# Gate rows and the mLSTM heads' row of gate sums made by DMA through device memory in place of products with the identity and with ones

## The chip, the core and the metric

The kernel runs on one core of one Trainium2 chip, in float32 throughout. Its engines work side by side, each through its own queue in program order: TensorE (PE, with its weight load PEld), VectorE (DVE), ScalarE (ACT), GpSimd (POOL) and SyncE (SP). They wait for each other by semaphores. The metric is the device time of one execution in microseconds (us). The kernel before takes 2371.95 us, the median of 3 runs (2371.75 to 2374.5).

## What is computed

Two transformer blocks in a row, each with two layers, on 256 tokens of width 1024. Cut to what the change touches:

```python
# first block, layers 0 and 1
ada = silu(c) @ w_ada[l] + b_ada[l]              # one row of 6 x 1024 values
sh1, sc1, g1, sh2, sc2, g2 = split(ada, 6)
h = layer_norm(ALPHA * h + g1 * mixer(u))        # g1 is one row, the same for all tokens
h = layer_norm(ALPHA * h + g2 * swiglu(u))
# in the mixer's mLSTM, per head, per direction
b = cumsum(log_sigmoid(f_pre))                   # over the tokens
log_d = where(tri, b[:, None] - b[None, :] + i_pre[None, :], NEG)
m_t = max(log_d.max(-1), b + m);  s = q @ k.T * exp(log_d - m_t)
# second block: an attention layer ("attn") and a GLA layer ("gla")
x = x + g1 * rms_norm(y);  x = x + g2 * rms_norm(mlp(x))    # attn also with g1x, g2x for the context's 256 tokens
```

Two things are needed in a layout in which they are not made. The gates `g1`, `g2` (`g1x`, `g2x`) are made as columns, 128 partitions by 8 values, and are needed as one row of 1024 values that is the same on all 128 partitions. For the mLSTM, `i - b` (4 heads, 2 directions, 256 tokens) is made with the tokens on the partitions and is needed as a row over the tokens, the same on all partitions.

## The kernel before

All work of the program stands in one SBUF area, `arena`, and eight PSUM banks. It goes through four stages: `layer 0`, `layer 1`, `attn`, `gla`. In each, TensorE runs the projections one panel of weights after the other. SyncE loads the panels (1 MB halves) into a ring of seven, each as soon as TensorE has freed a slot; GpSimd loads the pieces of `w_ada` (1 MB) into two slots, as VectorE uses them up. VectorE makes the gates by products with these pieces (`ada_turn`) between its other work. The order on every engine is written out by hand, and all waits are on counts.

- **Gate rows.** `gate_row` on TensorE (L631 to L639) makes one row: for each half, four 128x128 products of a column, repeated over 128 columns, with the identity `ident`, into one bank. On ScalarE `gate_row` (L1455 to L1460) copies each half from its bank into `grow`. There are ten rows: `g1` and `g2` in each of the two layers, `g1`, `g1x`, `g2`, `g2x` in `attn`, `g1` and `g2` in `gla`.
- **Where they stand on TensorE.** In a layer `g1` comes after the eight QK tiles and ahead of the twelve AQK tiles, `g2` after the tile `W3 10` and ahead of the first `W2` product. In `attn` `g1` and `g1x` come after `VL` and ahead of `RK` (the rotation of the keys), `g2` and `g2x` after panel 6 of the MLP's first half. In `gla` `g1` comes after the transposes `GH 3` and ahead of the wait for their drain by VectorE, `g2` after panel 6 of the MLP.
- **mLSTM heads.** VectorE makes `i - b` and `b` in `aB` (after the tile `CS`, inside its loop over the eight convolutions) and, per head, `make_diag`: four products of the identity with a column of `aB`, 128x128 each. `pe_mini(h, 0)` (L643) multiplies `ones` with the 512 columns of `diag` into the bank `A h`, which is the row on all partitions; the products `S h` follow. `dve_mini(h, 0)` adds the masks to `A h` (128x1024) into `Am`, takes the maximum, and goes on to the probabilities `P h`, which TensorE transposes two AQK tiles later (`PTT h`). Step `s` of head `h` comes after AQK tile `2 h + 1, 3, 4, 5` for `s` = 0, 1, 2, 3.
- **ScalarE in a layer.** It runs one SiLU per convolution (`silu 0` to `silu 7`, L1567 to L1571). VectorE's convolution `n` waits for `silu n-2`, because `cbuf` has two places; `S 0` on TensorE waits for `silu 7`.

## Time and profile before

| | |
|---|---|
| median of 3 runs | 2371.95 us |
| span of the profiled execution, the whole of it that the profile shows | 2375.7 us |
| lowest and highest run | 2371.75, 2374.5 us |
| TensorE busy | 2290.8 us, 96% |
| VectorE busy | 1383.0 us, 58% |
| ScalarE busy | 503.5 us, 21% |
| GpSimd busy | 243.8 us, 10% |
| mean granted TensorE clock | 0.992 of full speed |
| bytes moved by DMA | 391 MB, 165 GB/s |

The profiled execution is one of its own; what lies around the span (start and end of the program) is not in it, and its time as a run is not given apart. A float32 product is two matmul records in the trace, a float32 transpose one, so the number of records of a group is twice the number of its products. The busy time of TensorE is modelled; the distance from the start of one group to the start of the next is the firmer measure of what a group costs.

### The profile page before, as it was taken

How to read it: one execution, taken by the hardware profiler on the slowest of the kernel's cores; microseconds unless marked ns; L12 is line 12 of the kernel's file. 1: busy time of each engine (PE TensorE's matmuls, PEld its weight loads, DVE VectorE, ACT ScalarE, POOL GpSimd, SP SyncE). 2: the span in 40 equal slices, each digit the busy share in tenths (PEclk: the TensorE clock that was granted, in tenths of full speed). 3: DMA queues.
4: the chain of work that ended last, by engine and by line, in shares of the span. 5: the costliest groups of instructions: out<-in, count | busy, mean ns of one | idle time of the engine just before them, and what ended most of it. 6: DMA issues, size and time to landing. Idle time of an engine off the chain costs nothing.

```text
span 2375.7 us, 29622 instructions
## 1 busy us (share of the span) xinstructions
PE 2290.8 (96%) x11910; PEld 1858.6 (78%) x11910; DVE 1383.0 (58%) x2532; ACT 503.5 (21%) x1083; POOL 243.8 (10%) x165
## 2 busy tenths in 40 slices
PE   7999999999999999999999998999999999989998
PEld 5888587799768886868987655588888887767987
DVE  5764334654746433377877666766566457765456
ACT  1222220110011223201011355322200023342200
POOL 0000001321000000013410000000000002001332
PEclk9999999999999999999999999999999999999999
DMA  9853438544475333575564301433333324344442
GB/s 393 329 216 107 159 122 308 193 166 165 179 289 196 107 142 124 193 267 194 195 222 169 109 36 36 138 120 123 133 118 124 115 86 163 124 151 169 157 172 80
DMA packets 163511, 391.34 MB, mean 165 GB/s; under 512 B 6448, under 2 KB 10928, under 8 KB 160560
## 3 DMA queue, kind: packets, MB, share of 16 engines
q1 hardware_dynamic: 136736, 285.03, 33.8%
q0 software_dynamic: 24080, 93.69, 11.0%
q10 hardware_dynamic: 2560, 10.72, 1.3%
q8 instruction: 96, 1.57, 0.3%
q14 instruction: 39, 0.32, 0.0%
HBM read 388.37 MB, written 1.05 MB: 164 GB/s over the span
## 4 chain that ended last, share of the span: by engine, by line
PE 87%; DVE 7%; ACT 2%; DMA 2%; issue 1%; SPq 0%; DVEq 0%; ACTq 0%
PE bank L548 86%; DVE arena L2088 3%; DVE arena L2094 2%; DMA arena<-in_w_ada 2%; PE bank L546 1%; ACT arena L1440 1%; ACT arena L1443 1%; DVE arena L2091 1%; DVE junk L2094 1%; DVE arena L2226 0%; DVE arena L3040 0%; SPq L3202 0%; SPq L3205 0%; ACT L1440 0%; DVE arena L2157 0%
## 5 line engine op out<-in xcount | busy, mean ns | idle before, releaser
L548 PE MATMUL bank<-arena 128*128 128x256 f32 (+5 forms) x11422 | 2235.4, 364 | 46.8 <-DVE arena L2088 17.8
L548 PEld LDWEIGHTS bank<-arena 128*128 128x128 f32 (+2 forms) x11422 | 1801.8, 190 | 467.5 <-issue 250.5
L2088 DVE TENSOR_TENSOR arena<-arena 128x1024 f32<-128x1024 f32 (+8 forms) x535 | 446.6, 849 | 237.2 <-PE bank L548 195.8
L1440 ACT ACTIVATE arena<-arena 128x512 f32<-128x512 f32 (+5 forms) x427 | 213.9, 522 | 811.5 <-DVE arena L2088 458.1
L2094 DVE SCALAR_TENSOR_TENSOR arena<-arena 128x1028 f32<-128x1028 f32 (+6 forms) x367 | 309.2, 859 | 97.0 <-DMA arena<-in_w_ada 76.7
L3280 POOL DMA_DIRECT2D arena<-in_w_ada x88 | 62.9, 715 | 1749.2 <-DVEq L2103 1728.5
L2088 DVE TENSOR_TENSOR arena<-arena,bank 128x256 f32<-128x256 f32 (+2 forms) x326 | 150.1, 485 | 157.4 <-PE bank L548 147.7
L1443 ACT ACTIVATE arena<-bank 128x512 f32<-128x512 f32 (+1 forms) x199 | 110.5, 596 | 462.9 <-PE bank L548 402.3
L2088 DVE TENSOR_TENSOR arena<-bank,arena 128x512 f32<-128x512 f32 (+3 forms) x103 | 69.7, 690 | 215.3 <-PE bank L548 193.3
L1440 ACT ACTIVATE arena<-bank 128x256 f32<-128x256 f32 (+1 forms) x121 | 50.2, 432 | 507.8 <-PE bank L548 507.1
L2094 DVE SCALAR_TENSOR_TENSOR arena<-bank,arena 128x254 f32<-128x254 f32 (+2 forms) x184 | 78.2, 469 | 51.1 <-PE bank L546 34.1
L2091 DVE TENSOR_SCALAR arena<-arena 128x512 f32<-128x512 f32 (+8 forms) x278 | 80.4, 322 | 20.7 <-ACT arena L1440 12.7
L546 PE MATMUL bank<-arena 128*128 128x128 f32 x488 | 64.1, 281 | 28.2 <-DVE arena L2091 16.9
L546 PEld LDWEIGHTS bank<-arena 128*128 128x128 f32 x488 | 57.4, 145 | 39.2 <-issue 22.9
L2094 DVE SCALAR_TENSOR_TENSOR junk<-arena 128x1028 bf16<-128x1028 f32 x64 | 78.7, 1229 | 14.5 <-DMA arena<-in_w_ada 10.1
L2094 DVE SCALAR_TENSOR_TENSOR arena<-arena,bank 128x512 f32<-128x512 f32 (+1 forms) x40 | 24.8, 645 | 99.1 <-PE bank L548 97.3
L1440 ACT ACTIVATE arena<-bank,arena 128x128 f32<-128x128 f32 (+2 forms) x138 | 57.5, 488 | 79.2 <-DVE arena L2088 24.4
L2091 DVE TENSOR_SCALAR arena<-bank,arena 128x256 f32<-128x256 f32 (+1 forms) x112 | 46.5, 468 | 47.2 <-PE bank L548 35.7
L3235 POOL TENSOR_TENSOR arena<-arena 128x1024 f32<-128x1024 f32 x20 | 50.7, 2535 | 116.7 <-PE bank L548 93.8
L1440 ACT ACT_TABLE_LOAD x48 | 61.6, 1283 | 4.2 <-PE bank L548 2.2
L3237 POOL TENSOR_TENSOR arena<-arena 128x1024 f32<-128x1024 f32 x20 | 53.0, 2649 | 1.6
L3250 POOL TENSOR_TENSOR arena<-arena 128x1024 f32<-128x1024 f32 x14 | 33.0, 2355 | 97.6 <-PE bank L548 82.3
(37 smaller groups left out, 222.2 us busy)
## 6 DMA issues: line engine op xcount, KB each, us to landing
arena<-in_w_ada POOLq DMA_DIRECT2D x88, 1028.0 KB, 5.6
arena<-in_w_in SPq DMA_DIRECT2D x84, 1024.0 KB, 7.3
arena<-in_w SPq DMA_DIRECT2D x56, 1024.0 KB, 6.4
arena<-in_w_mlp_in SPq DMA_DIRECT2D x32, 1024.0 KB, 6.5
arena<-in_w_mlp_out SPq DMA_DIRECT2D x32, 1024.0 KB, 6.4
arena<-in_w_gla SPq DMA_DIRECT2D x12, 1024.0 KB, 7.0
arena<-in_w_ada SPq DMA_DIRECT2D x16, 514.0 KB, 19.5
arena<-in_w_a SPq DMA_DIRECT2D x8, 1024.0 KB, 7.0
```

What stands on the lines that cost most here:

```text
L546: ins = nc.tensor.transpose(out, lhsT, rhs)
L548: ins = nc.tensor.matmul(out, lhsT, rhs, start=start, stop=stop)
L1440: return nc.scalar.activation(out, x, f, **kw)
L1443: return nc.scalar.activation(out, tile(key)[:, :out.free_size()], f)
L2088: return V.tensor_tensor(out, x, y, op)
L2091: return V.tensor_scalar(out, x, s1, s2, op0, op1) if op1 is not None else V.tensor_scalar(out, x, s1, None, op0)
L2094: return V.scalar_tensor_tensor(out=out, in0=x, scalar=s, in1=y, op0=op0, op1=op1, **kw)
L3235: nc.gpsimd.tensor_tensor(up_sum(at), a21, a22, ALU.add).then_inc(up_sums_made, 1)
L3237: nc.gpsimd.tensor_tensor(a21, a11, a21, ALU.subtract).then_inc(up_sums_made, 1)
L3250: nc.gpsimd.tensor_tensor(wsum, a21, a22, ALU.add).then_inc(mlp_sums_made, 1)
L3280: pool.dma_start(adaw[:, n % ADA_SLOTS], half_source(job, q)).then_inc(ada_in[n % ADA_SLOTS], 16)
```

## The change

The ten `gate_row`s are gone from TensorE and ScalarE, and so are `make_diag`, `diag` and the eight products with `ones`. In their place ScalarE's queue issues DMAs:

- `row_to_dram` stores the columns of a gate, 128 partitions by 8 values, into a row of `gate_rows` in device memory, as 1024 pieces of 4 bytes.
- `row_to_all`, later on the same queue, waits until that has landed and loads the row of 4 KB into all 128 partitions of `grow` (512 KB).
- For the mLSTM one DMA stores 16 columns of `aB` (2048 pieces of 4 bytes) into `decay_rows` after `silu 2`. After `silu 4` ScalarE waits for its landing and loads the 8 KB into all partitions of `DR` (1 MB), which lies in the area of `VA`. `aB` is laid out so that its first half is those 16 columns.

VectorE waits for `decay_in` ahead of the first head, adds the masks to `DR` in place of the bank, and waits for `row_in` where it waited for ScalarE's drains.

```diff
@@ -333,7 +346,8 @@
 
         gz = area(M["GATE"], NT, 16)
         gw = area(M["GATE"] + 32, 4, 32)
-        aB = area(M["GATE"] + 160, 2, 2, NT, 4)
+        aB = area(M["GATE"] + 160, 2, M_HEADS, 2 * NT).rearrange("p a h (d t) -> p a d t h", d=2)
+        decay_cols = area(M["GATE"] + 160, 4 * M_HEADS)
         small = area(M["GATE"] + 192, 16, 4)
         var, newton = area(M["GATE"] + 240, NT), area(M["GATE"] + 242, NT)
         W = M["WORK"]
...
-            def gate_row(key, cols, stage=None):
-
-                for half in range(2):
-                    ps = open_tile(f"{key} {half}")
-                    pe.wait_ge(dve_of[stage or Progress.phase], DV.of(stage or Progress.phase, "next " + key if stage else key))
-                    for j in range(4):
-                        col = cols[:, 4 * half + j:4 * half + j + 1]
-                        mm(ps[:, j * P:j * P + P], col.to_broadcast([P, P]), ident, done=f"{key} {half}" if j == 3 else None)
-
             def pe_mini(h, s):
 
                 if s == 0:
-                    pe.wait_ge(dve_done, DV.at(f"diag {h}"))
-                    ps = open_tile(f"A {h}")
-                    mm(ps[:, :], ones, diag[:, :, :].rearrange("p a b -> p (a b)"), done=f"A {h}")
                     pe.wait_ge(act_done, AC.at("silu 7"))
                     ps = open_tile(f"S {h}")
...
 
-            def gate_row(key, x):
-
-                for half in range(2):
-                    act.wait_ge(pe_done, PE.at(f"{key} {half} full"))
-                    drain(f"{key} {half}", grow[:, x, PW * half:PW * half + PW]).then_inc(
-                        act_done, AC.drained(f"{key} {half}"))
+            def row_to_dram(stage, key, cols, made_in=None):
+
+                act.wait_ge(dve_of[made_in or stage], DV.of(made_in or stage, "next " + key if made_in else key))
+                act.dma_start(gate_rows[GATE_ROWS.index((stage, key))].rearrange("(k p) -> p k", p=P), cols,
+                              allow_slow_non_contiguous=True).then_inc(row_out, 16)
+
+            def row_to_all(stage, key, x, last=None):
+
+                act.wait_ge(row_out, rows_by(stage, last or key))
+                act.dma_start(grow[:, x, :], gate_rows[GATE_ROWS.index((stage, key))].partition_broadcast(P)).then_inc(row_in, 16)
 
             def context_root(tt):
@@ -1564,12 +1555,20 @@
                 func(gw[:, 1, :], gw[:, 0, :], ACT.Exp, scale=-1.0).then_inc(act_done, AC.step())
                 act.wait_ge(act_done, AC.count)
                 func(gw[:, 2, :], gw[:, 1, :], ACT.Ln, bias=1.0).then_inc(act_done, AC.step("softplus"))
+                row_to_dram(stage, "g1", adac[:, 2, :])
                 for n in range(8):
                     act.wait_ge(dve_done, DV.at(f"conv {n}"))
                     func(QK[:, 2 * n:2 * n + 2, :].rearrange("p a b -> p (a b)"),
                         cbuf[:, 2 * (n % 2):2 * (n % 2) + 2, :].rearrange("p a b -> p (a b)"), ACT.Silu).then_inc(
                         act_done, AC.step(f"silu {n}"))
-                gate_row("g1", 0)
+                    if n == 2:
+                        act.wait_ge(dve_done, DV.at("decays"))
+                        act.dma_start(decay_rows[l].rearrange("(c p) -> p c", p=P), decay_cols,
+                                      allow_slow_non_contiguous=True).then_inc(decay_out, 16)
+                    if n == 4:
+                        row_to_all(stage, "g1", 0)
+                        act.wait_ge(decay_out, 16 * (l + 1))
+                        act.dma_start(DR.rearrange("p h s -> p (h s)"), decay_rows[l].partition_broadcast(P)).then_inc(decay_in, 16)
                 for n in range(12):
                     x, m = (AQ, n) if n < 6 else (AK, n - 6)
...
+                    if p == 1:
+                        row_to_dram(stage, "g2", adac[:, 5, :])
+                    if p == 3:
+                        row_to_all(stage, "g2", 1)
                 act.wait_ge(dve_done, DV.at("up 3"))
                 act.wait_ge(pe_done, PE.at("W1 10 full"))
                 drain("W1 10", sg[:, 2, :], ACT.Silu).then_inc(act_done, AC.drained("W1 10"))
-                gate_row("g2", 1)
 
...
                         context_root(tt)
+                    row_to_dram("attn", "g1", adac[:, 2, :], stage)
+                    row_to_dram("attn", "g1x", adacx[:, 2, :], stage)
                 first_product(0)
                 if l == DEPTH - 1:
...
-            gate_row("g1", 0)
-            gate_row("g1x", 1)
+            row_to_all("attn", "g1", 0, "g1x")
+            row_to_all("attn", "g1x", 1)
 
...
             def attn_extra(p):
+                if p == 4:
+                    row_to_dram("attn", "g2", adac[:, 5, :])
+                    row_to_dram("attn", "g2x", adacx[:, 5, :])
                 if p == 6:
-                    gate_row("g2", 0)
-                    gate_row("g2x", 1)
+                    row_to_all("attn", "g2", 0, "g2x")
+                    row_to_all("attn", "g2x", 1)
 
...
+            row_to_dram("gla", "g1", adac[:, 2, :])
             gk(0)
             gq(0)
             for h in range(G_HEADS):
+                if h == 1:
+                    row_to_all("gla", "g1", 0)
                 if h + 1 < G_HEADS:
                     gk(h + 1)
...
             gg(3)
-            gate_row("g1", 0)
...
+                if p == 4:
+                    row_to_dram("gla", "g2", adac[:, 5, :])
                 if p == 6:
-                    gate_row("g2", 1)
+                    row_to_all("gla", "g2", 1)
 
...
-            def make_diag(h):
-
-                if h:
-                    dve.wait_ge(pe_done, PE.at(f"A {h - 1} full"))
-                for j in range(4):
-                    ts(diag[:, j, :], ident, aB[:, 0, j // 2, j % 2, h:h + 1], None, ALU.mult).then_inc(
-                        dve_done, DV.step(f"diag {h}" if j == 3 else None))
-
             def dve_mini(h, s):
 
                 if s == 0:
-                    dve.wait_ge(pe_done, PE.at(f"A {h} full"))
-                    ps = tile(f"A {h}")
-                    row = ps[:, :].rearrange("p (d s) -> p d s", d=2).unsqueeze(2).to_broadcast([P, 2, NT, T])
-                    tt_(Am[:, :, :, :], row, masks[:, :, :, :], ALU.add).then_inc(dve_done, DV.drained(f"A {h}"))
+                    dve.wait_ge(dve_done, DV.count)
+                    row = DR[:, h, :].rearrange("p (d s) -> p d s", d=2).unsqueeze(2).to_broadcast([P, 2, NT, T])
+                    tt_(Am[:, :, :, :], row, masks[:, :, :, :], ALU.add).then_inc(dve_done, DV.step())
                     dve.wait_ge(dve_done, DV.count)
                     V.reduce_max(small[:, 0, :].rearrange("p (d t) -> p d t", d=2), Am[:, :, :, :], AX.X).then_inc(
                         dve_done, DV.step())
...
-                    if h + 1 < M_HEADS:
-                        make_diag(h + 1)
                     dve.wait_ge(pe_done, PE.at(f"S {h} full"))
                     ps = tile(f"S {h}")
                     dve.wait_ge(act_done, AC.at(f"exp {h}"))
...
+                        marks[Progress.phase, "dve", "decays"] = DV.count
                     if turns[0] < 20:
                         ada_turn(turns.pop(0), [("ada", 0)])
                 if l == 0:
@@ -2631,9 +2632,8 @@
                         tt_(crow[:, i, :D], crow[:, i, :D], csig[i], ALU.mult).then_inc(
                             dve_done, DV.step("conds" if i == 2 else None))
                     dve.wait_ge(masks_in, 16)
-                dve.wait_ge(dve_done, DV.count)
-                make_diag(0)
                 dve.wait_ge(act_done, AC.at("silu 7"))
+                dve.wait_ge(decay_in, 16 * (l + 1))
                 for n in range(12):
...
+                dve.wait_ge(row_in, rows_by(stage, "g1"))
                 for half in range(2):
...
-                dve.wait_ge(act_done, AC.at("g2 1 drained"))
+                dve.wait_ge(row_in, rows_by(stage, "g2"))
```

## Rows read from the trace of the kernel before

**Rows 1.** The page: busy time of each engine; the chain that ended last, by engine.
```profile
PE 2290.8 (96%) x11910; PEld 1858.6 (78%) x11910; DVE 1383.0 (58%) x2532; ACT 503.5 (21%) x1083; POOL 243.8 (10%) x165
PE 87%; DVE 7%; ACT 2%; DMA 2%; issue 1%; SPq 0%; DVEq 0%; ACTq 0%
```
**Rows 2.** The chain, in order of time: start us, us, what, number of records.
```profile
185.85 18.19 PE bank L548 x82
204.04 0.87 PE bank L546 x8
...
223.97 15.59 PE bank L548 x72
...
1195.99 93.00 PE bank L548 x522
...
1308.39 35.88 PE bank L548 x178
...
1552.37 192.25 PE bank L548 x896
...
2184.20 82.47 PE bank L548 x736
```
**Rows 3.** Timeline of ScalarE, attn: first and last of four half rows; idle, releaser last.
```profile
1333.88 0.60 ACT L1443 ACTIVATE arena<-bank 128x512 f32<-128x512 f32 x1 [0.29 <-PE bank L548]
...
1336.56 0.60 ACT L1443 ACTIVATE arena<-bank 128x512 f32<-128x512 f32 x1 [0.29 <-PE bank L548]
```
**Rows 4.** Timeline of VectorE, attn: its last gate product, the rotated keys.
```profile
1334.93 0.08 DVE L2094 DVE_READ_ACCUMULATOR arena<-arena 128x1 f32 x1
1337.48 0.69 DVE L2088 TENSOR_TENSOR arena<-bank,arena 128x512 f32<-128x512 f32 x1 [2.47 <-PE bank L548]
```
**Rows 5.** Timelines of ScalarE and VectorE, gla: g1's last half, post row, GH 3's drain.
```profile
2128.97 0.60 ACT L1443 ACTIVATE arena<-bank 128x512 f32<-128x512 f32 x1 [0.29 <-PE bank L548]
2128.98 0.34 ACTq L2065 DMA_DIRECT2D arena<-in_post  x1
...
2127.38 0.88 DVE L2094 SCALAR_TENSOR_TENSOR arena<-bank,arena 128x256 f32<-128x256 f32 x2 [3.07 <-ACT arena L1443]
```
**Rows 6.** Timeline of ScalarE, layer 0: silu 2, 4, 5, 7; drain of AQK 1.
```profile
104.29 0.63 ACT L1440 ACTIVATE arena<-arena 128x512 f32<-128x512 f32 x1 [7.50 <-DVE arena L2094]
...
118.58 0.63 ACT L1440 ACTIVATE arena<-arena 128x512 f32<-128x512 f32 x1 [6.52 <-DVE arena L2094]
125.73 0.63 ACT L1440 ACTIVATE arena<-arena 128x512 f32<-128x512 f32 x1 [6.52 <-DVE arena L2094]
...
140.04 0.63 ACT L1440 ACTIVATE arena<-arena 128x512 f32<-128x512 f32 x1 [6.52 <-DVE arena L2094]
...
149.94 0.66 ACT L1440 ACTIVATE arena<-bank 128x256 f32<-128x256 f32 x2 [6.27 <-PE bank L548]
```
**Rows 7.** Timelines of VectorE and PE, layer 0: convolution 7, Am, P 0, PTT 0.
```profile
135.38 1.00 DVE L2091 TENSOR_SCALAR arena<-bank,arena 128x256 f32<-128x256 f32 x2 [0.23 <-DVE arena L2094]
...
150.87 1.23 DVE L2088 TENSOR_TENSOR arena<-bank,arena 128x1024 f32<-128x1024 f32 x1 [5.07 <-PE bank L548]
...
158.34 0.88 DVE L2094 SCALAR_TENSOR_TENSOR arena<-arena 128x256 f32<-128x256 f32 x2
...
166.19 0.60 PE L546 MATMUL bank<-arena 128*128 128x128 f32 x4
```
**Rows 8.** The page: DMA queues (packets, MB, share of 16 engines); issues, us to landing.
```profile
q1 hardware_dynamic: 136736, 285.03, 33.8%
q0 software_dynamic: 24080, 93.69, 11.0%
...
arena<-in_w_in SPq DMA_DIRECT2D x84, 1024.0 KB, 7.3
...
arena<-in_small SPq DMA_DIRECT2D x1, 29.0 KB, 20.0
```
**Rows 9.** Windows, layer 0: busy PE, PEld, DVE, ACT, POOL; clock, DMA share, GB/s.
```profile
110.00:120.00 10.00, 10.00 (x47) 8.71 (x47) 9.60 (x21) 1.26 (x2) 0.71 (x1) 1.00 0.95 370
```

More of the change, by code:

```diff
@@ L212, in minis, with rows_by @@
     return [(h, s) for h in range(M_HEADS) for s, lag in ((3, 5), (2, 4), (1, 3), (0, 1)) if n == 2 * h + lag]
+GATE_ROWS = [("layer 0", "g1"), ("layer 0", "g2"), ("layer 1", "g1"), ("layer 1", "g2"), ("attn", "g1"), ("attn", "g1x"),
+             ("attn", "g2"), ("attn", "g2x"), ("gla", "g1"), ("gla", "g2")]
+def rows_by(stage, key):
+    return 16 * (GATE_ROWS.index((stage, key)) + 1)
 class Progress:
@@ L276, in program @@
         small_in, par2_in = sem("small_in"), sem("par2_in")
+        row_out, row_in = sem("row_out"), sem("row_in")
+        decay_out, decay_in = sem("decay_out"), sem("decay_in")
+        gate_rows = nc.dram_tensor("gate_rows", (len(GATE_ROWS), D), F32).ap()
+        decay_rows = nc.dram_tensor("decay_rows", (DEPTH, 4 * PW), F32).ap()
         PE, AC, DV = (Progress(n, marks) for n in ("pe", "act", "dve"))
@@ L343, in program @@
         hn = area(W + 2048, NT, T)
-        diag = area(W + 2560, 4, P)
+        DR = area(M["VA"], M_HEADS, PW)
         cbuf = area(W, 4, T)
@@ L1120, in _ @@
             release(w_kv)
-            gate_row("g1", adac[:, 2, :], last)
-            gate_row("g1x", adacx[:, 2, :], last)
             pe.wait_ge(par2_in, 16)
@@ L1255, in attn_seam @@
                 evicted("Y", range(2, 4))
[L1257 to L1262 removed]
+            fast_mlp("mlp", 0, T, attn_seam)
             normed_transposes("next", dg_next, range(2), None)
@@ L2863, in fast_mlp @@
                         tiles_, rows_used, sem_, count, _, _ = post
-                        dve.wait_ge(act_done, AC.at("g2x 1 drained" if tiles_ == 4 else "g2 1 drained"))
+                        dve.wait_ge(row_in, rows_by(Progress.phase, "g2x" if tiles_ == 4 else "g2"))
                         dve.wait_ge(sem_, count)
@@ L2992, in _ @@
                 ada_turn(q, [("ada", 1), ("adax", 2)])
-            dve.wait_ge(act_done, AC.at("g1x 1 drained"))
+            dve.wait_ge(row_in, rows_by("attn", "g1x"))
             dve.wait_ge(dve_done, DV.count)
@@ L3174, in _ @@
                         dve_done, DV.drained(f"GH {h}" if ft else None))
-            dve.wait_ge(act_done, AC.at("g1 1 drained"))
+            dve.wait_ge(row_in, rows_by("gla", "g1"))
             dve.wait_ge(dve_done, DV.count)
```

16 lines of the change are left out of this document (2 added, 14 removed).

## Prediction

> **What bounds the kernel now.** I read the busy times first: TensorE is busy 96% of the span, VectorE 58%, ScalarE 21%, and the chain that ended last lies on TensorE for 87% of its length and on DMA for 2% [rows 1]. Then the chain in order of time, to see whether TensorE leads at the places that the change touches [rows 2]. It does in long unbroken pieces. The pairs 18.19 + 0.87 are the mLSTM heads, the 93.00 us from 1195.99 hold layer 1's `g2`, the 35.88 us from 1308.39 hold `g1` and `g1x` of attn, the 192.25 us from 1552.37 `g2` and `g2x`, and the 82.47 us from 2184.20 gla's `g2`. A product taken out of such a piece shortens the run by its whole time, unless whoever is waited for next was just on time. That is what the timelines are read for.
>
> **What the change removes.** *Price of a gate row.* A half row is four products of 128x128. In attn four halves run one behind the other; ScalarE drains them as they come, at 1333.88 and so on to 1336.56 [rows 3], so a half takes (1336.56 - 1333.88) / 3 = 0.893 us and a row 1.79 us. *Price of a product with `ones`.* A piece of the heads with no such product has 72 records in 15.59 us, 0.2165 us each; the piece with one has 82 records in 18.19 us, of which 80 are of the same kind [rows 2]. 18.19 - 80 x 0.2165 = 0.87 us. There are eight, four heads in two layers: 6.96 us.
>
> *Which rows come back whole.* In the layers four rows, 7.15 us. Layer 0's `g1` stands between QK and AQK: `silu 7` is over at 140.67 and `S 0`, the first to need it, follows AQK 1, drained at 149.94 [rows 6], so TensorE can come 1.79 us earlier and meets nobody. `g2` of layer 1 stands in 93.00 us of TensorE alone, which run on over the first half of the down products [rows 2]; layer 0 runs the same code with less on VectorE. In attn four rows, 7.15 us. `g1`, `g1x` are followed by `RK`; VectorE ends its gate products at 1334.93 + 0.08 and then waits 2.47 us, until 1337.48, for `RK` [rows 4]. Without the rows `RK` is there at some 1333.9, VectorE starts on it at 1335.0, and TensorE goes on with query 0, which needs neither; the 3.57 us come back whole. `g2`, `g2x` lie inside 192.25 us of TensorE alone [rows 2]. gla's `g2`, 1.79 us, likewise.
>
> *Which does not.* gla's `g1` hides a wait. VectorE drains `GH 3` from 2127.38 to 2128.26, and the last half of `g1` is full at 2128.97 [rows 5]. TensorE then needs `GH 3`. With the row gone it waits until 2128.3 in place of 2128.95: 0.65 us of the 1.79 come back. The load of the post row, issued at 2128.98, moves ahead of the two drains, and nothing else follows.
>
> Sum: nine rows at 1.79 (16.1), one at 0.65, eight products at 0.87 (6.96): **23.7 us**. ScalarE also loses twenty drains of 0.60 us, beside TensorE, so nothing. VectorE loses 32 products for `diag`, beside TensorE as well. Its addition of the masks, 1.23 us [rows 7], reads SBUF in place of a bank; I take it unchanged. It may start before `S h`, which only adds slack.
>
> **What the change adds.** *Loads to all partitions.* Twelve, ten of 0.5 MB and two of 1 MB, 7 MB against 391 MB. On ScalarE a load of this kind costs 0.34 us of issue [rows 5], and it lands like a panel, in 7.3 us [rows 8]. Every user comes tens of us later (`row_in` is waited for at the first residual or late in the MLP). Nothing. They share the DMA engines with the weights at shares up to 0.95 [rows 9], but the panel ring is seven deep and TensorE shows no wait for it. The chain has 2% on DMA [rows 1], the pieces of `w_ada`; 7 MB more is 1.8% more bytes, so 0 to 1 us. I take 0.
>
> *Stores in pieces of 4 bytes.* No row shows such a store. Its issue on ScalarE costs 0.34 us [rows 5] at least, and at most as long as the store takes. Its landing I bound from packets. The queue of the panels had 136736 packets in 33.8% of 16 engines' 2375.7 us, 0.094 us each; the software queue 24080 in 11.0%, 0.174 us each [rows 8]. The gate sums are 2048 pieces, 128 an engine. Low end: a panel of 1 MB, 7.3 us. At 0.094 us a piece: 12 us. High end, where each piece waits for one packet of either other queue: 128 x 0.36 = 46 us. I take 12 us, since the share of the engines at the time leaves gaps, and keep 46. Below nothing it can't be: it replaces no transfer.
>
> *The new wait.* Behind it on ScalarE stand `silu 5` to `silu 7`, and behind these VectorE's convolutions and `S 0`. The store is issued at the end of `silu 2`, 104.9; ScalarE gets to the wait at 119.2, after `silu 4`; `silu 5` comes at 125.73 [rows 6]. A landing within 14 us costs nothing at all. Convolution 7 starts at 135.38 [rows 7] and needs `silu 5`; with 0.63 us for it and two issues, ScalarE may wait until some 134, 29 us after the store. After that convolution 7 and `silu 7` slip, and `silu 7` has from 140.67 to about 148.1 (149.94 less 1.8), 7.5 us more. So TensorE loses only what the landing takes **beyond 36.7 us**. The load into `DR` then lands at about 149, and `P 0` takes from 150.87 to 159.22 and is wanted at 166.19 [rows 7], 2.7 us earlier in the changed kernel: later than this, so it does not bind first. Layer 1 has the same loop; I take the same slack. At 12 us the cost is 0, at 46 us 2 x 9.3 = 18.6 us.
>
> The gate rows' stores are half as many pieces and are waited for two silus or two MLP panels later or more: never late where the other is not. Issued on ScalarE, they stand ahead of work with several us of idle time before it, as the 6.52 us before each SiLU [rows 6].
>
> The Trainium skill, page "Perfetto Trace Analysis", section "DMA Optimizations", speaks against the stores: DMAs under 2 KB have a significant overhead each. No row here shows one; with the high end of 46 us the time would be 2366.9 us. The page "DMA: Bandwidth & Descriptors", section "Measured (HBM→SBUF, 128 partitions, SWDGE, issued from GpSimd)", has about 10.5 ns for a small packet; an estimate by it is 1.3 us over a fixed part for 128, which leaves the sum at 23.7.
>
> Profiled execution: 2375.7 - 23.7 = 2352.0. It lies 3.7 us above the median of the runs, and I take that offset as unchanged: 2371.95 - 23.7 = **2348.3 us**.
>
> **The rivals.** *A, the gain is partly swallowed at seams.* Where attn and gla hand over between the halves of an MLP, the chain passes through VectorE, and if VectorE leads there, the four rows of attn and gla's `g2` come back as waits: 5 x 1.79 = 8.9 us less, 2357.2. For it: 7% of the chain is VectorE's [rows 1]. Against it: it waits 2.47 us right behind `g1x` [rows 4], and `g2` lies in unbroken TensorE time.
>
> *B, the stores are slow, but bearable.* Landing between 36.7 and 48 us, or an issue that holds ScalarE as long in gla's heads, where it is in the chain: up to all of the gain, in the middle about 2360. For it: a load of only 29 KB took 20.0 us to land behind others [rows 8], and the engines are 95% busy just then [rows 9]. Against it: that load stood behind a start-up queue on its own ring.
>
> *C, slower than before: the wait for `decay_out` stops ScalarE, and TensorE waits at `S 0` for `silu 7`, in both layers.* Price 2 x (landing - 36.7). It eats the 23.7 us at a landing of 48.5 us, 0.38 us a piece, and decides for slower from there; at 0.47 us a piece (60 us) the time is 2371.95 - 23.7 + 46.6 = 2394.9. For it: the engines' share of 0.95 at the wait [rows 9]; against it: it needs more than one packet of each other queue between any two pieces.
> By the Trainium skill, "DMA: Bandwidth & Descriptors", section "Queues, rings and completion order", an engine goes round the queues and takes a whole packet from each; were every piece a packet of its own among full queues, that is the high end of 46 us, short of C.
>
> **How the numbers follow.** Forecast 0.75 (2344 to 2352 by itself, for the rounding of the prices and 0 to 1 us of DMA), A 0.10, B 0.10, C 0.05. The range from 2344 to 2358 holds the forecast, A and about a third of B, with the rest of B and C left out. A measurement of this kernel can tell some 0.2% from no change, 4.7 us. Faster by more: forecast, A and most of B, 0.92. Within: 0.03, the end of B. Slower: C and nothing else, 0.05.
>
> **What would show it.** Right: TensorE has 176 fewer records (160 of the rows, 16 with 512 columns), its busy time is down by some 23 us and its idle time up by 1 us at most; the head period falls from 19.06 to 18.2 us; ScalarE reaches `silu 5` within a few us of `silu 4`; VectorE's first addition of masks in a layer no longer waits for a bank; in gla TensorE idles 1.1 us before the first mix tile. Wrong: a gap of ScalarE between `silu 4` and `silu 5` of over 15 us, TensorE idle before `S 0` (B, C); TensorE idle growing at the seams of attn or before `scores 0` (A); long DMA issues on ScalarE's queue.

## The result, and the profile after

The changed kernel takes **2359.11 us** (median of 5 executions, 2356.3 to 2364.93) against 2373.25 us before (5 executions): a ratio of 0.9945, 95% interval 0.9934 to 0.9956. By the ratio it is faster by 13.1 us (10.4 to 15.7), by the two medians by 14.1, and not by the 23.7 of the forecast; 2359.11 lies 1.1 us above the range.

The page after, busy times and waits of TensorE (us in total, how many, the longest). (Lines have moved: L562, L560 are the products of L548, L546; VectorE's L2099, L2102, L2105 are L2088, L2091, L2094; ScalarE's L1427, L1430 are L1440, L1443.)

```profile
span 2357.3 us, 29223 instructions
PE 2267.6 (96%) x11734; PEld 1838.6 (78%) x11734; DVE 1375.0 (58%) x2500; ACT 492.3 (21%) x1063; POOL 243.4 (10%) x165
...
PE bank L562 <- DVE arena L2099: 17.4, 11, 3.0
...
PE bank L560 <- DVE arena L2099: 3.9, 1, 3.9
```

TensorE has 176 records fewer and is busy 23.2 us less than in [rows 1]. Its idle time, span less busy, went from 84.9 to 89.7 us. The wait of 3.9 us is new. It is in gla's first head; the chain of the kernel before runs there on TensorE for 92.92 us on end, and the chain after goes another way. Start, us and what, first before, then after:

```profile
1950.25 92.92 PE bank L548 x392
```
```profile
2000.70 2.40 DVE arena L2105 x4
...
2003.44 13.13 DMA arena<-in_w_ada
...
2016.60 2.40 DVE arena L2105 x4
...
2025.74 1.09 PE bank L560 x4
```

The timelines of ScalarE's queue, GpSimd, VectorE and TensorE at this place (start, us, and in brackets the idle time before), after and then, of GpSimd and VectorE, before:

```profile
1998.47 0.38 ACTq L1445 DMA_DIRECT2D gate_rows<-arena  x1
...
2000.91 0.72 POOL L3281 DMA_DIRECT2D arena<-in_w_ada  x1 [11.23 <-DVEq L2114]
...
2012.95 1.23 DVE L2105 SCALAR_TENSOR_TENSOR arena<-arena 128x1028 f32<-128x1028 f32 x1 [9.87 <-DMA arena<-in_w_ada]
...
2016.60 1.23 DVE L2105 SCALAR_TENSOR_TENSOR arena<-arena 128x1028 f32<-128x1028 f32 x1 [1.26 <-DMA arena<-in_w_ada]
...
2025.74 1.79 PE L560 MATMUL bank<-arena 128*128 128x128 f32 x6 [3.93 <-DVE arena L2099]
```
```profile
2022.27 0.72 POOL L3280 DMA_DIRECT2D arena<-in_w_ada  x1 [11.23 <-DVEq L2103]
...
2027.50 1.23 DVE L2094 SCALAR_TENSOR_TENSOR arena<-arena 128x1028 f32<-128x1028 f32 x1 [3.06 <-DMA arena<-in_w_ada]
...
2030.35 1.23 DVE L2094 SCALAR_TENSOR_TENSOR arena<-arena 128x1028 f32<-128x1028 f32 x1 [0.46 <-DMA arena<-in_w_ada]
```

ScalarE stores gla's `g1` at 1998.47. The piece of `w_ada` that GpSimd asks for 2.4 us later is there only at 2012.93, 12.0 us after its issue; in the kernel before the same piece took 5.2 us (issued 2022.27, there at 2027.48). VectorE stands still for 9.87 us instead of 3.06, and for the next piece 1.26 instead of 0.46, so its part of head 0 is late, and TensorE waits.

What the DMA engines did meanwhile, by windows (us, busy PE, PEld, DVE, ACT, POOL; clock, DMA share, GB/s). First the kernel after: the store, the time behind it, and the recovery; then the kernel before with its piece:

```profile
1999.00:2001.00 2.00, 2.00 (x6) 0.81 (x5) 1.85 (x5) 0.00 (x0) 0.09 (x1) 1.00 0.24 2
...
2004.00:2010.00 6.00, 6.00 (x29) 5.28 (x28) 0.00 (x0) 0.38 (x1) 0.16 (x1) 1.00 0.73 38
2010.00:2014.00 4.00, 4.00 (x20) 3.52 (x19) 1.05 (x1) 0.00 (x0) 0.00 (x0) 1.00 0.95 381
```
```profile
2025.00:2029.00 4.00, 4.00 (x20) 3.51 (x19) 1.50 (x3) 0.39 (x1) 0.52 (x1) 1.00 1.02 407
```

The packets of the store itself are over by 2001: the queue view from 1998 to 2004 has 1040 of them (1024 pieces and 16 more of 4 bytes) in 8.0% of 16 engines' 6 us, 0.007 us each. Yet from 2004 to 2010 the engines are "busy" for 0.73 of the time and move 38 GB/s, a tenth of the 407 that they move in the kernel before at full share. A high share does not say that bytes flow: from 2004 to 2010 there are 56 read packets in 73.1% of 16 engines' 6 us, 1.25 us each, where one of the kernel before takes 0.16 from 2025 to 2029. The same stands behind the larger store of the gate sums in layer 0, which lands at 116.25, after and then before:

```profile
110.00:116.00 6.00, 6.00 (x29) 5.23 (x29) 5.13 (x11) 0.63 (x1) 0.71 (x1) 1.00 0.78 34
116.00:120.00 4.00, 4.00 (x21) 3.48 (x20) 3.50 (x8) 0.36 (x1) 0.00 (x0) 1.00 0.93 306
```
```profile
110.00:116.00 6.00, 6.00 (x29) 5.23 (x29) 5.67 (x13) 0.63 (x1) 0.71 (x1) 1.00 1.03 405
```

So here the reads are slow until the store has landed, and fast again right behind it. For gla's store the trace of the changed kernel has no landing; that of `gates_only`, the kernel below with the ten rows' DMAs alone, has one. The store is issued at 2007.54, its packets are over by 2010, and it lands at 2017.63, 10.1 us after its issue. The windows before and behind that:

```profile
2014.00:2017.60 3.60, 3.60 (x19) 3.16 (x18) 0.00 (x0) 0.06 (x1) 0.00 (x0) 1.00 0.90 35
...
2020.00:2022.00 2.00, 2.00 (x11) 1.77 (x10) 0.00 (x0) 0.00 (x0) 0.00 (x0) 1.00 0.97 380
```

In layer 0 the slow reads cost TensorE nothing. ScalarE's timeline, layer 0, answers [rows 6]:

```profile
119.64 0.63 ACT L1427 ACTIVATE arena<-arena 128x512 f32<-128x512 f32 x1 [7.16 <-DVE arena L2105]
119.65 0.34 ACTq L1451 DMA_DIRECT2D arena<-gate_rows  x1
120.03 0.46 ACTq L1571 DMA_DIRECT2D arena<-decay_rows  x1
130.42 0.63 ACT L1427 ACTIVATE arena<-arena 128x512 f32<-128x512 f32 x1 [10.14 <-DVE arena L2105]
```

The load into `DR` is issued right behind `silu 4`: the new wait for `decay_out` cost nothing, the store had landed 11.5 us after its issue. The load itself takes 13.6 us, not the 7.3 of the forecast, and still lands long before it is needed. `silu 5` is 3.6 us further from `silu 4` than before, because VectorE waited 3.52 us for a piece of `w_ada`. `silu 7`, at 145.2, is still ahead of `S 0`.

**A figure used below.** Executions differ in mean granted clock, and the time follows it: over 44 executions of the kernel before, beside all the runs below, the time rises by 2.4 us for each 0.001 that the mean clock is lower. So beside the median the table gives the *time at full clock*, time less (1 - mean clock) x span, median over the executions. The clock of an execution is given to 0.001, 2.4 us, so this figure scatters by 1 to 2 us from one execution to the next.

| kernel | executions | median us | ratio to before (95%) | mean clock | at full clock | TensorE's gap in gla's head 0 |
|---|---|---|---|---|---|---|
| before | 44 | 2372.2 | 1 | 0.9934 | 2357.3 | none |
| changed, both series | 11 | 2361.8 | 0.9945, 0.9949 | 0.9907 | 2339.9 | 3.9; 5.5 |
| `gates_only` | 5 | 2362.9 | 0.9966 (0.9954 to 0.9978) | 0.9910 | 2342.8 | 4.0 |
| `row_only` | 12 | 2368.3 | 0.9983 (0.9975 to 0.9992) | 0.9930 | 2351.1 | none |
| `no_stores` | 4 | 2350.4 | 0.9912 (0.9899 to 0.9925) | 0.9928 | 2334.1 | none |
| `gla_g1_no_store` | 6 | 2352.4 | 0.9910 (0.9893 to 0.9927) | 0.9920 | 2334.0 | none |
| `gla_g1_late` | 4 | 2351.3 | 0.9910 (0.9893 to 0.9926) | 0.9922 | 2333.7 | none |
| `packed`, `packed_again` | 9 | 2352.9 | 0.9917, 0.9922 | 0.9914 | 2332.0 | none |
| `packed_gates` | 4 | 2353.9 | 0.9921 (0.9906 to 0.9936) | 0.9912 | 2332.7 | none |
| pieces 8, 16, 32, 64 bytes apart | 18 | 2351.6 | 0.9909, 0.9908, 0.9913, 0.9903 | 0.9925 | 2333.9 | none |
| `one_partition` | 5 | 2361.0 | 0.9948 (0.9932 to 0.9964) | 0.9916 | 2340.7 | 1.0 |
| `double` | 6 | 2406.5 | 1.0124 (1.0096 to 1.0153) | 0.9830 | 2363.5 | 17.0 |

### The profile page after: what moved, and what is told of

Same layout as the page of the kernel before. It is cut to its first block, busy times and chain, and to the rows that moved or that the text cites. A ratio compares the mean times of both kernels' runs of the same rounds, so it can differ in the third digit from the quotient of the medians.

```text
span 2357.3 us, 29223 instructions
## 1 busy us (share of the span) xinstructions
PE 2267.6 (96%) x11734; PEld 1838.6 (78%) x11734; DVE 1375.0 (58%) x2500; ACT 492.3 (21%) x1063; POOL 243.4 (10%) x165
## 4 chain that ended last, share of the span: by engine, by line
PE 87%; DVE 8%; ACT 2%; DMA 1%; issue 1%; SPq 0%; DVEq 0%; ACTq 0%
PE bank L562 85%; DVE arena L2099 4%; DVE arena L2105 3%; PE bank L560 1%; DMA arena<-in_w_ada 1%; ACT arena L1427 1%; ACT arena L1430 1%; DVE junk L2105 1%; DVE arena L2102 1%; DVE arena L3041 1%; DVE arena L2237 0%; ACT L1427 0%; SPq L3203 0%; DVE arena L2168 0%; SPq L3195 0%
## 5 line engine op out<-in xcount | busy, mean ns | idle before, releaser
L562 PE MATMUL bank<-arena 128*128 128x256 f32 (+5 forms) x11246 | 2211.2, 365 | 49.1 <-DVE arena L2099 17.4
L562 PEld LDWEIGHTS bank<-arena 128*128 128x128 f32 (+2 forms) x11246 | 1781.4, 190 | 466.2 <-issue 248.0
L2099 DVE TENSOR_TENSOR arena<-arena 128x1024 f32<-128x1024 f32 (+7 forms) x543 | 455.0, 853 | 231.5 <-PE bank L562 186.1
L1427 ACT ACTIVATE arena<-arena 128x512 f32<-128x512 f32 (+5 forms) x427 | 213.7, 522 | 811.1 <-DVE arena L2099 464.0
L2105 DVE SCALAR_TENSOR_TENSOR arena<-arena 128x1028 f32<-128x1028 f32 (+6 forms) x367 | 309.0, 859 | 105.2 <-DMA arena<-in_w_ada 85.8
L2099 DVE TENSOR_TENSOR arena<-arena,bank 128x256 f32<-128x256 f32 (+2 forms) x326 | 150.1, 485 | 157.9 <-PE bank L562 148.5
L1430 ACT ACTIVATE arena<-bank 128x512 f32<-128x512 f32 (+1 forms) x179 | 99.4, 596 | 451.1 <-PE bank L562 407.3
L2099 DVE TENSOR_TENSOR arena<-bank,arena 128x512 f32<-128x512 f32 (+2 forms) x95 | 59.9, 645 | 173.7 <-PE bank L562 154.9
L1427 ACT ACTIVATE arena<-bank 128x256 f32<-128x256 f32 (+1 forms) x121 | 50.2, 432 | 508.2 <-PE bank L562 507.5
L2105 DVE SCALAR_TENSOR_TENSOR arena<-bank,arena 128x254 f32<-128x254 f32 (+2 forms) x184 | 78.1, 469 | 73.4 <-PE bank L560 34.1
L560 PE MATMUL bank<-arena 128*128 128x128 f32 x488 | 65.0, 283 | 31.0 <-DVE arena L2102 16.6
L560 PEld LDWEIGHTS bank<-arena 128*128 128x128 f32 x488 | 57.8, 146 | 42.5 <-issue 21.4
L2105 DVE SCALAR_TENSOR_TENSOR junk<-arena 128x1028 bf16<-128x1028 f32 x64 | 78.7, 1229 | 13.9 <-DMA arena<-in_w_ada 9.6
L2102 DVE TENSOR_SCALAR arena<-arena 128x256 f32<-128x256 f32 (+8 forms) x246 | 74.0, 327 | 19.3 <-ACT arena L1427 12.7
L2105 DVE SCALAR_TENSOR_TENSOR arena<-arena,bank 128x512 f32<-128x512 f32 (+1 forms) x40 | 24.8, 645 | 99.7 <-PE bank L562 97.9
L2102 DVE TENSOR_SCALAR arena<-bank,arena 128x256 f32<-128x256 f32 (+1 forms) x112 | 46.5, 468 | 51.3 <-PE bank L562 38.1
L1427 ACT ACTIVATE arena<-bank,arena 128x128 f32<-128x128 f32 (+2 forms) x138 | 57.5, 486 | 83.8 <-PE bank L560 23.7
```

The lines of the kernel that those rows point to most:

```text
L560: ins = nc.tensor.transpose(out, lhsT, rhs)
L562: ins = nc.tensor.matmul(out, lhsT, rhs, start=start, stop=stop)
L1427: return nc.scalar.activation(out, x, f, **kw)
L1430: return nc.scalar.activation(out, tile(key)[:, :out.free_size()], f)
L2099: return V.tensor_tensor(out, x, y, op)
L2102: return V.tensor_scalar(out, x, s1, s2, op0, op1) if op1 is not None else V.tensor_scalar(out, x, s1, None, op0)
```

## The experiments

Theory S: a store in pieces of 4 bytes slows the reads from device memory behind it, and who waits for those is late. Its rivals are the loads to all partitions, the layers, and a long profiled execution of before.

**One part alone.** `gates_only` keeps the diagonals and the products with `ones` and has no DMA of the gate sums; `row_only` is the kernel before with those products in DMAs, and the ten rows on TensorE. Of `gates_only`:

```diff
+                    mm(ps[:, :], ones, diag[:, :, :].rearrange("p a b -> p (a b)"), done=f"A {h}")
...
-                        act.dma_start(decay_rows[l].rearrange("(c p) -> p c", p=P), decay_cols,
```

> The ten gate rows by DMA, the mLSTM row left on TensorE with its diagonals. Theory S (the stores in pieces of 4 bytes slow the DMA reads that follow them for some 10 us, and what waits for those reads is late): the ten rows take 17.8 us of TensorE away, and the gap of 3.9 us in gla's first head with what follows it gives 4 to 6.5 us back, so 2373.3 - 17.8 + 5 = about 2360 to 2362, and VectorE still waits about 10 us for a piece of w_ada in gla. Theory R (the missing gain is spent in the layers, at the mLSTM row's load and the later SiLUs): about 2355.5, with all the gain of the ten rows.

> Only the mLSTM row by DMA, the ten gate rows left on TensorE and ScalarE. Theory S: the eight products come back whole, 6.9 us, since nothing on TensorE waits for the slowed reads in the layers: about 2366.4. Theory R: 2370 or more, with TensorE idle in the layers.

Measured: `gates_only` 2362.9, with VectorE's wait at 10.7 us and the gap at 4.0. (The 17.8 us of the expectation are ten rows at 1.78; the prediction gave the ten 16.7, as gla's `g1` comes back by 0.65 alone.) `row_only` 2368.3, 3.6 us under before by the medians and 6.2 at full clock, for 6.9 forecast. So the layers do not eat the gain, and the shortfall comes with the gate rows. The two do not add up exactly: at full clock `gates_only` gains 14.5 us and `row_only` 6.2, 20.7 together, where the changed kernel has 17.4; what makes the 3.3 us is open.

**Without stores, and with one store left out.** `no_stores` has no store at all; `gla_g1_no_store` lacks the line `row_to_dram("gla", "g1", ...)` alone, and its load reads attn's row. Of `no_stores`:

```diff
-                act.dma_start(gate_rows[...].rearrange("(k p) -> p k", p=P), cols, ...)
-                act.wait_ge(row_out, ...)
+                act.dma_start(grow[:, x, :], a["post"][x].partition_broadcast(P)).then_inc(row_in, 16)
```

> The changed kernel without any store of gates or of gate sums; its loads to all partitions stay, at the same places, and read inputs of the same size, so the values are not the reference's. Theory S: the pieces of w_ada in gla land in 5.4 us again instead of 12, TensorE's gap in gla's first head is gone, and the time is 2352.5 to 2355. Theory L (the loads to all partitions, 7 MB, are what costs): no change, 2359. Theory O (the gain is smaller only because the profiled execution of before was a long one): no change, 2359.

> The changed kernel without one store, that of gla's g1; the load takes attn's g1 row, so the values are not the reference's. If this store alone costs (theory S with its place: two pieces of w_ada land in 12 to 13 us instead of 5.4, VectorE is 9.9 us late, TensorE idles 3.9 us in gla's first head and the clock falls there): 4 to 7 us less than the changed kernel, 2352 to 2355. If the other nine stores and the two of the gate sums take as much: 2 us less or none, 2357 to 2359.

> The changed kernel once more, beside the next three, for the spread of its executions and their mean granted clock. If the clock is lower in it than in the kernel before by more than chance, it is near 0.991 again (0.9935 is the mean of 17 executions of before) and the time near 2359; if the first five executions fell low by chance, the mean clock comes to 0.993 and the time to about 2355.

Measured: without any store 2350.4, 8.7 us under the changed kernel and a little under the expected 2352.5 to 2355, with all twelve loads in place; so the loads cost nothing that shows (23.2 us gained at full clock, 23.7 forecast). With the one store of gla's `g1` left out and the other eleven there, 2352.4, beside 2363.2 of the changed kernel in the same series: 10.8 us hang on this store. The changed kernel's second series had the clock of the first (0.9907 and 0.9908), and its gap was 5.5 us behind a wait of VectorE of

```profile
2019.73 1.23 DVE L2105 SCALAR_TENSOR_TENSOR arena<-arena 128x1028 f32<-128x1028 f32 x1 [11.86 <-DMA arena<-in_w_ada]
```

**The same store at another time.**

```diff
-            row_to_dram("gla", "g1", adac[:, 2, :])
             gk(0)
...
                 if h == 1:
-                    row_to_all("gla", "g1", 0)
+                    row_to_dram("gla", "g1", adac[:, 2, :])
+                if h == 3:
+                    row_to_all("gla", "g1", 0)
```

> The changed kernel with one store moved: gla's g1 is stored at head 1 (some 33 us later) and loaded at head 3. Nothing else differs and the values are the reference's. Theory S with its place: the reads are slowed for 10 us at a time in which VectorE waits for no piece of w_ada, so the 3.9 to 5.5 us of TensorE's gap and the lower clock around it are gone: 2352 to 2355, as without that store. If the store costs wherever it stands: 2359 to 2363.

Measured: 2351.3, slightly under the expected range. The store comes 36 us later and costs nothing there, as GpSimd loads the next piece only 8.7 us later (in 5.9 us) and VectorE is not waiting for it. VectorE's wait at the old place:

```profile
2009.10 1.23 DVE L2106 SCALAR_TENSOR_TENSOR arena<-arena 128x1028 f32<-128x1028 f32 x1 [3.18 <-DMA arena<-in_w_ada]
```

**Twice as many pieces.** Each store once more, into rows of its own.

> Every store in pieces of 4 bytes twice, the second into rows of its own. Theory S with a price for each piece (about 6.6 us of delay for 1024 pieces): the pieces of w_ada in gla land in 18 to 22 us, TensorE idles 10 to 14 us in gla's first head, the gate sums land in 20 to 24 us and the layers lose 0 to 5 us each: 2368 to 2380. If a store costs a fixed time whatever its pieces or overlaps itself: 2359 to 2362.

Measured: 2406.5, far above the expected 2368 to 2380. In gla the step is as expected: a first piece of `w_ada` in 23.9 us, VectorE's wait, TensorE's gap, and the window behind the stores with 29 GB/s:

```profile
2045.48 1.23 DVE L2109 SCALAR_TENSOR_TENSOR arena<-arena 128x1028 f32<-128x1028 f32 x1 [21.72 <-DMA arena<-in_w_ada]
...
2059.46 1.79 PE L560 MATMUL bank<-arena 128*128 128x128 f32 x6 [16.97 <-DVE arena L2103]
...
2025.00:2042.00 17.00, 17.00 (x66) 12.02 (x64) 0.00 (x0) 0.38 (x1) 0.00 (x0) 1.00 0.86 29
```

What was not expected is ScalarE's queue in layer 0, and TensorE's wait for it:

```profile
108.71 0.37 ACTq L1568 DMA_DIRECT2D decay_rows<-arena  x1
109.11 11.94 ACTq L1570 DMA_DIRECT2D decay_rows<-arena  x1
...
123.43 21.12 ACTq L1453 DMA_DIRECT2D arena<-gate_rows  x1
...
154.84 1.15 ACT L1427 ACTIVATE arena<-arena 128x512 f32<-128x512 f32 x2 [30.79 <-DMA decay_rows<-arena]
...
160.93 14.45 PE L562 MATMUL bank<-arena 128*128 128x256 f32 x59 [10.79 <-ACT arena L1427]
```

The second store's issue holds ScalarE for 11.94 us and the next DMA's for 21.12, the second store lands after 45.3 us, and this is the forecast's rival C at work. The reads do not slow down there: the 4096 pieces go out between the packets of the others, from 112 to 156, and the engines move 320 GB/s and more from 120 to 150; the pieces of `w_ada` land in 10.4 to 11.2 us.

```profile
130.00:140.00 10.00, 10.00 (x47) 8.72 (x47) 9.61 (x20) 0.00 (x0) 0.71 (x1) 1.00 1.02 325
```

So the number of pieces alone does not slow the reads. In gla the 2048 are out within 2.5 us of their issue, in layer 0 of the changed kernel within 8; whether it is this burst that makes the difference, no run varied alone. The clock falls with the pauses, to 0.983 in the mean, and that alone makes 25 us against before: (0.9934 - 0.9830) x 2390.

**As many pieces, further apart.** The columns of the target are spread: its last dimension is 16 for pieces 64 bytes apart, and 8, 4 and 2 for 32, 16 and 8 bytes. The loads read inputs, as in `no_stores`; in gla the load comes over 40 us after the store, so this does not touch the piece behind it.

```diff
-        gate_rows = nc.dram_tensor("gate_rows", (len(GATE_ROWS), D), F32).ap()
+        gate_rows = nc.dram_tensor("gate_rows", (len(GATE_ROWS), D, 16), F32).ap()
```

> As many pieces of 4 bytes, issued at the same places, but each 64 bytes from the next in device memory; the loads read inputs of the same size, so the values are not the reference's. If the slowing comes with the number of pieces: 2357 to 2360, pieces of w_ada in 12 us in gla as in the changed kernel. If it comes from neighbouring pieces that are written into the same stretch of device memory by different engines: like the kernel without stores, 2350 to 2353, and w_ada in 5.4 us.

> As the run with pieces 64 bytes apart, but 32 bytes apart: two pieces of 4 bytes in each 64 bytes. The loads read inputs, so the values are not the reference's. If what costs is that several pieces fall into one stretch of 64 bytes, already two of them: pieces of w_ada in gla over 8 us, time 2354 to 2360. If it grows with the number of pieces in a stretch (16 in the changed kernel, 2 here), or the stretch is of 32 bytes or less: pieces of w_ada within 6.5 us and 2350 to 2354.

> Pieces of 4 bytes 16 bytes apart, four in each 64 bytes; the loads read inputs, so the values are not the reference's. If the slowing grows with the number of pieces in a stretch (16 in the changed kernel gave 6.6 to 8.6 us more on a w_ada piece, 2 gave none): between 0 and 3 us more, time 2350 to 2354. If there is a threshold between 16 and 32 bytes: as the changed kernel, pieces of w_ada in 12 us, 2359.

> Pieces of 4 bytes 8 bytes apart, eight in each 64 bytes; the loads read inputs, so the values are not the reference's. If the slowing grows with the number of pieces in a stretch: a piece of w_ada in gla in 7 to 10 us, VectorE's wait for it 5 to 7 us, time 2352 to 2358. If only pieces that touch each other are slow: 5.4 us and 2350 to 2354.

Measured: 2352.2, 2351.2, 2350.9, 2350.5. Still 1024 pieces of 4 bytes each, and in gla no slow reads down to 16 bytes (5.3 to 5.5 us for the piece of `w_ada`; in layer 0, behind 2048 pieces, 9.2 to 9.7, for 8.2 in `packed` and before). VectorE's wait in gla for pieces 64, 32, 16 and 8 bytes apart:

```profile
2005.69 1.23 DVE L2105 SCALAR_TENSOR_TENSOR arena<-arena 128x1028 f32<-128x1028 f32 x1 [3.31 <-DMA arena<-in_w_ada]
...
2002.49 1.23 DVE L2105 SCALAR_TENSOR_TENSOR arena<-arena 128x1028 f32<-128x1028 f32 x1 [3.18 <-DMA arena<-in_w_ada]
...
2004.80 1.23 DVE L2105 SCALAR_TENSOR_TENSOR arena<-arena 128x1028 f32<-128x1028 f32 x1 [3.11 <-DMA arena<-in_w_ada]
...
2008.01 1.23 DVE L2105 SCALAR_TENSOR_TENSOR arena<-arena 128x1028 f32<-128x1028 f32 x1 [4.32 <-DMA arena<-in_w_ada]
```

At 8 bytes it begins (the piece of `w_ada` in 6.5 us in gla and 12.4 in layer 0; 6.5 in gla for itself says little, `row_only` has it there with no store), at 4 bytes, side by side, it is 12.0 and 14.0 us. The stores themselves land sooner too: 2048 gate sums 16 bytes apart in 5.7 and 6.0 us, 8 bytes apart in 7.9 and 9.2, side by side in 11.5 and 12.5 (13.4 twice in the second series).

**Who writes the neighbours.** The pieces stay 4 bytes and side by side, but the 8 (or 16) neighbours come from one partition:

```diff
-                ...rearrange("(k p) -> p k", p=P), cols, ...
+                ...rearrange("(p k) -> p k", p=P), flat48[:, at:at + 16:2], ...
```

> As many pieces of 4 bytes as in the changed kernel, into as few bytes of device memory, but neighbours come from one partition: each partition writes its 8 (or 16) values side by side, taken from every other column so that each stays a piece of its own; the values are not the reference's. If the slowing comes from different DMA engines writing next to each other at the same time: 2350 to 2354, pieces of w_ada in under 6.5 us in gla. If it comes from many pieces in one stretch of device memory, whoever writes them: 2357 to 2363, 12 us or more.

Measured: 2361.0. In gla the piece takes 9.6 us and the gap is 1.0; in layer 0 the two pieces behind the store take 21.7 and 18.8 (15.8 and 15.6 in the changed kernel, 18.6 and 18.8 in its second series), VectorE waits 7.3 us, and TensorE 2.8 us for ScalarE. So that different partitions write next to each other is not the whole of it; neither expectation is met in full.

The landing of the store orders all of these. In gla, us from the issue to the landing:

| gla's `g1` store | the store | the piece of `w_ada` issued 2.4 us behind it |
|---|---|---|
| `packed`, 128 pieces of 32 bytes | 1.4 | 5.4 |
| 64, 32, 16 bytes apart | 2.7, 2.6, 3.2 | 5.5, 5.3, 5.3 |
| 8 bytes apart | 4.8 | 6.5 |
| `one_partition` | 7.3 | 9.6 |
| `gates_only`, side by side | 10.1 | 12.9 |

Where the store takes longer than 4 us, the piece lands 4.1 to 5.2 us behind it. What keeps a store open for so long after its packets is not shown; and layer 0 of `double`, with fast reads beside a store that is open for 45 us, says that an open store is not enough by itself.

**Fewer, whole pieces.** The rows of `w_ada` that make the gates are laid out so that partition `p` holds the values 8p to 8p + 7; a gate goes out as 128 pieces of 32 bytes, the gate sums as 128 of 64, and VectorE reads `DR` with a stride. `packed_gates` does it for the gates alone.

```diff
-                act.dma_start(gate_rows[...].rearrange("(k p) -> p k", p=P), cols, ...)
+                act.dma_start(gate_rows[...].rearrange("(p k) -> p k", p=P), cols)
-                        act.dma_start(decay_rows[l].rearrange("(c p) -> p c", p=P), decay_cols, ...)
+                        act.dma_start(decay_rows[l].rearrange("(p c) -> p c", p=P), decay_cols)
```

> The same DMAs with whole pieces for each partition: the rows of w_ada that make the gates are laid out so that a partition's eight values are neighbours (128 pieces of 32 bytes), and the gate sums are stored 64 bytes a partition and read by VectorE with a stride, in two additions a head. Theory S, by the number of pieces: like the kernel without stores, 2352.5 to 2355.5, w_ada pieces in 5.4 to 6 us in gla. If the slowing comes with any store to device memory, whatever its pieces: 2359. If the strided addition is dear: VectorE's additions of the masks take over 2 us in place of 1.23, still beside TensorE.

> The gate rows stored as 128 pieces of 32 bytes, the gate sums in pieces of 4 bytes as in the changed kernel. If the stores of the gate sums cost the run nothing (rivals B and C off): as with everything packed, 2352 to 2354, and silu 7 still 4 to 5 us late in both layers. If they cost through the pieces of w_ada and the SiLUs of the layers: 2355 to 2359.

> The kernel with pieces of 32 and 64 bytes once more, for its spread and mean clock. 2351 to 2354; mean clock 0.9915 to 0.9925 if the clock is lower without the gate rows on TensorE for another reason than the slowed reads, 0.993 or more if the first four executions were low by chance (then 2349).

Measured: 2352.6, 2353.9 and 2353.6. `packed` is the better version that the runs point to, with `gla_g1_late` beside it: both beat both kernels, and their difference is within the spread. Gate sums land in 2.1 us (2.5 and 2.7 in `packed_again`), and VectorE's two strided additions take 1.95 us, beside TensorE:

```profile
144.40 1.95 DVE L2097 TENSOR_TENSOR arena<-arena 128x512 f32<-128x512 f32 x2
```

`packed_gates` has `silu 7` at 145.1 as the changed kernel has, and no loss: the slowed reads of the layers cost the run nothing.

## Why the prediction was wrong, and where it was right

**The removal was right.** At full clock the kernels without the slowed reads of gla stand at 2333.7 (45 executions; 2332.0 to 2334.1 by the rows of the table), 23.6 us under before; the forecast was 23.7. The pieces of the chain after show the prices of products with `ones`, against 18.19 in [rows 2]:

```profile
164.57 17.33 PE bank L562 x80
181.90 0.87 PE bank L560 x8
```

18.19 - 17.33 = 0.86 a head, forecast 0.87, and a head period of 18.20. The pieces with gate rows, again against [rows 2]:

```profile
1181.65 92.84 PE bank L562 x506
...
1294.25 33.94 PE bank L562 x146
...
1535.20 187.00 PE bank L562 x864
...
2167.91 80.68 PE bank L562 x720
```

gla's `g2` gives 82.47 - 80.68 = 1.79, as forecast. The others seem to give 0.16, 1.94 and 5.25 for forecasts of 1.79, 3.57 and 3.57. The windows tell why (columns as above), the kernel after and then before, at the starts of these pieces:

```profile
1182.00:1186.00 4.00, 4.00 (x23) 4.00 (x23) 1.99 (x4) 0.42 (x1) 3.92 (x2) 0.58 0.13 51
1294.50:1298.50 4.00, 4.00 (x23) 4.00 (x23) 0.83 (x4) 2.24 (x7) 0.00 (x0) 0.57 0.00 0
```
```profile
1196.00:1200.00 4.00, 4.00 (x36) 4.00 (x37) 3.39 (x7) 0.84 (x2) 3.90 (x2) 1.00 0.23 93
1308.50:1312.50 4.00, 4.00 (x34) 3.96 (x35) 1.16 (x6) 2.91 (x9) 0.00 (x0) 1.00 0.00 0
1553.50:1557.50 4.00, 4.00 (x12) 3.17 (x12) 3.86 (x4) 0.00 (x0) 0.00 (x0) 0.57 0.00 0
```

After a pause of 2.5 us the clock stands at 1.2 GHz for 3.4 us, which costs 1.7: in the first two pieces of after, in the third of before. With 1.7 added or taken off they give 1.9, 3.6 and 3.5. In gla, `g1` hid VectorE's drain as told: TensorE now idles 1.16 us there, forecast 1.1. Rival A is off; the waits at the seams are those of before (17.4 us in 11 waits, 17.8 before).

**The landing came out right by luck.** Taken 12 us, measured 11.5 and 12.5. The sum took 0.094 us for a piece, from a queue of large packets; the store's own packets take 0.015 us each (2064 in 15.4% of 16 engines' 12.5 us, from 104.5 to 117) and in gla 0.007. At that rate the 128 pieces of an engine are 2 us. In layer 0 the last of them is over 8.0 us after the issue, and the landing comes 3.5 us later still. The wait for `decay_out` cost nothing, as forecast. The price of the wait beyond 36.7 us has one test, and not a clean one, as the issues hold ScalarE too, `double`: landings of 45.3 and 39.2 us give 8.6 + 2.5 = 11.1 us by that rule; TensorE's waits for ScalarE's L1427 grew by 20.5 - 7.3 = 13.2.

**The step that failed** is "Stores in pieces of 4 bytes". It priced the store by who waits for *it*, bounded by how long its own packets queue, and said of the gate rows' stores "never late where the other is not". It did not ask what the store does to the others. The notes on the loads had looked for the panel ring and found it seven deep; the pieces of `w_ada` have two slots, and that VectorE waits 3.06 us for such a piece in gla's head 0 already before the change was not looked up. In its place the runs showed 3.9 and 5.5 us of TensorE's time there, and 10.8 us of the whole on this one store. That head had 3.7 us of room: 6.8 and 0.8 us more of VectorE's waits for two pieces became 3.9 us of TensorE's. The sentence on the loads, "The chain has 2% on DMA", had the same blind spot: it priced bytes. The store's own place decides: moved by 36 us it is free. Rival B had the place (gla's heads) and the time (2360) but the wrong carrier, ScalarE's issue, which is 0.38 us.

By the Trainium skill, page "DMA: Bandwidth & Descriptors", section "Specifications", a transfer below 512 bytes makes the DMA engine read, modify and write. The trace agrees with a hidden cost of small pieces, but size alone is not it: in gla pieces of 4 bytes 16 bytes apart and pieces of 32 bytes slow nobody. That the slow stretch is such work on one stretch of memory is my reading, not shown.

**The offset was misread, without effect on the 2348.3**, which is the median less the gain; it enters the 2352.0 for the profiled execution alone (measured 2357.3). The span of before lay 3.7 us above the median and this was taken as a constant. But a span is shorter than its own execution, by 1.8 us (2357.3 and 2359.11 in the changed kernel), so the profiled execution of before was 5.5 us longer than the median. Its clock of 0.992, under the mean of 0.9934, makes some 3.3 of them; the rest is scatter and rounding. A profile's clock has to be held against the runs' before its own time is used.

**What the forecast left out is the clock.** At full clock the changed kernel gains 17.4 us: 23.6 less 6.2 for the slowed reads. Over both series its time gains 10.4 (2372.2 - 2361.8), and the difference of 7 is (0.9934 - 0.9907) x 2360 = 6.4 and rounding. Half of that goes with the slowed reads. In the kernels without them the clock is 0.9921 in the mean (45 executions), and behind the gap of 3.9 us the changed kernel shows

```profile
2025.00:2032.00 7.00, 6.25 (x26) 5.67 (x27) 4.87 (x9) 0.98 (x2) 0.00 (x0) 0.51 0.45 173
```

The other half, 0.0013 or 3.1 us, is there in the kernels without gate rows on TensorE (means from 0.9912 to 0.9930). It is as much as two stretches at 1.2 GHz cost, and the profiles have two candidates: behind the pauses at 1181 and 1294 the clock falls in 13 and 14 of the 15 profiles of such kernels, and in neither of the two with gate rows (before, `row_only`), though the pauses are as long (2.5 and 2.2 to 2.6 us). Why the same pause lowers the clock in one kernel and not in the other is open; no run varied it alone, and two profiles on one side are few. The lower clock, wherever it falls, is the reason that the kernels without slowed reads stand at 2351.7 and not at 2348.5 (2372.2 - 23.7).

## What to carry to other kernels

Price a small store twice: by who waits for it, and by what every read behind it loses until it has landed (10 to 13 us here, for pieces of 4 bytes side by side), and look for the shallowest buffer (here two slots of `w_ada`), not the deepest. Lay a column out so that each partition writes its values as one piece, or put the store where no consumer stands at a read. A DMA share near 1 is worth nothing without the GB/s beside it.

## What the runs showed of the hardware

- 1024 stores of 4 bytes side by side are over by packets within 2.5 us, land after 10.1 us, and hold reads down to 35 and 38 GB/s, from 407, until then; 2048 of them in `double` to 29 GB/s for 17 us. At 16 bytes apart they land in 3.2 us and the reads of gla are as fast as without them.
- 4096 such pieces that go out between full queues over 44 us (`double`, layer 0) leave the reads at 320 GB/s and more.
- Behind one unfinished store of 2048 pieces issuing a second on ScalarE took 11.9 us, and behind both a load 21.1 us; in the changed kernel no issue of these DMAs took more than 0.80.
- A pause of TensorE of 2.5 us can cost 1.7 us more than its length, by 3.4 us at 1.2 GHz behind it, or nothing more. The mean clock of kernels with pauses as long differed by 0.0013, 3.1 us.
